# Attention's bias added by VectorE from tables with reversed keys, and the transfers around it in another order

## The chip, the cores and the metric

One core of a Trainium2 chip. The metric is the device time of one launch in microseconds (us), here the median of several runs. Engines: TensorE (matmuls, and weight loads beside them), VectorE, ScalarE, GpSimd, and SyncE, which issues most of the DMA transfers; ScalarE issues the others in its own instruction stream. The engines run side by side and order themselves by semaphores.

## The reference, cut to what matters

One layer of a streaming encoder for 256 prompt tokens and 32 sample tokens, width 1024, float32. Each group has its own conditioning vector c; `silu(c) @ w_ada + b_ada` gives six rows (shift, scale and gain, for the mixer and for the experts). The mixer projects `h = x * (1 + s1) + b1` with one matrix w_in (1024 x 2048) to three groups of heads:

```python
# A: 4 heads, chunks of 64, all earlier chunks in reach, clipped relative bias
logits = einsum(q, k) * HEAD_DIM**-0.5 + table[clip(rel, -128, 128) + 128]
logits = where(band_valid, logits, NEG_INF); p = softmax(logits); o = p @ v
# B: 8 query heads on 2 key heads, window of own chunk + 128 keys, sinks
logits = einsum(q, k) * HEAD_DIM**-0.5 + t5_table[t5_bucket(rel)]
m = max(max(logits), sink); e = exp(logits - m); p = e / (sum(e) + exp(sink - m))
# C: GLU, causal depthwise conv of width 31, LayerNorm, swish
```

The sample group attends to cached keys and values and its own 32. The groups' outputs go through w_out, then residual and LayerNorm. Keys, values and the end of the convolution's input are outputs too. Then comes a mixture of 32 experts (top 4 of 32, w_e_in 1024 x 2048 and w_e_out 1024 x 1024 for each expert, float32), residual and LayerNorm.

## The kernel before, in words

*The start.* SyncE issues twelve w_ada pieces of 2 MB (`ada_unit`, L369; six pairs of two halves, four ring slots at first, later two), w_in in five transfers on the other half of the big tile `w`, and small rows. After the first piece of each pair it issues b_ada as one transfer of 128 KB: each of four 256-column quarters copied to 32 partitions. TensorE multiplies a piece (`ada`, L1393), VectorE adds b_ada (`add_mod`, L923). The first four pieces give scale and shift of the mixer; they are transposed and put into `modc` by four chained copies (L954). Thirteen projections of 128 columns and three for the values follow (L1485); the other pieces of w_ada stand among them, the fifth after the sixth projection. VectorE runs the convolution beside this.

*The bias tables.* VectorE copies the transposed tables (L915), GpSimd extends them to rows of 512 relative positions (L538 to L541), ScalarE writes these to DRAM and reads them back in ten transfers with one element's shift a partition (L649 to L654): partition p holds the bias row beginning at element p. With keys in rising order the partitions come out in reversed order. So the bias enters the logits through a matmul: `anti` (a reversed identity; `anti32` for the sample, by blocks of 32) times the table (L1549, L1555), with start=True, and q*k is added on top of it in PSUM (L1553, L1564). GpSimd builds `anti` and `anti32` at the start.

*The attention.* 15 steps (`ATT`): for token tile 0 two of A and four of B (steps 0 to 5, 128 keys, two heads a step), the same for tile 1 (steps 6 to 11, 256 keys), and three for the sample (12 to 14, four heads in one tile). The text calls the first six short steps, the next six long steps. For one step the work goes: logits (TensorE) -> maxima (VectorE, L1062 or L1065) -> exps (ScalarE, L727, reads the logits in PSUM and writes `prob`, in `hb`) -> normalise (VectorE, L1087) -> transposes of the probabilities (TensorE, L1581) -> copy_pT (ScalarE, L740) -> values (TensorE, L1597) -> copy_o (VectorE, L1093). `prob` has two slots. The loops, each engine's instructions in this order:

```python
# TensorE: logits 0, 1, 2; then for s in 0..14:
#   transpose_p(s); logits(s+3) for s < 5, none for s = 5, logits(s+2) from 6; values(s); out_proj part from s = 6
# ScalarE: exps(0), exps(1); then copy_pT(s); exps(s+2)
# VectorE: maxima 0, 1, 2; normalise(0); then copy_o(s-1); normalise(s+1); maxima of the step whose logits came
```

The output projection (L1633) stands in parts among steps 6 to 14 (`OP_AFTER`), six matmuls of 512 columns (as two passes each where the profile counts them) in steps 6 to 9.

Before exps(0) ScalarE copies the last values, stores rows of the conditioning to DRAM (`store_mod`, L656), and then issues ten transfers: eight of values and keys (L702 to L710, shown as L700) and two of the convolution's end (L713).

*SyncE's order around it.* When all projections are done, four loads of expert 0 (`load`, L430, shown as L406); then a wait for the two transfers of the convolution's end, for st_mod and others; then six transfers that broadcast gain, scale and shift rows (L438, L440), four more loads of expert 0, and the copies of the caches to the outputs. Two loads of expert 1 follow when the attention is done, expert 0's w_e_out (L409) when the output projection is done, and more from then on, in a ring of 20 slots of 1 MB, as blocks of experts come to an end.

*The experts.* 51 blocks of 32 token slots: gather (L1746), w_e_in (L1766), activation, w_e_out (L1795), combine (L1729).

Of the kernel before, what the change touches and what calls it, by code (L numbers as in the profile page):

```python
# [10 lines left out]
ALU = mybir.AluOpType  # L11
ACT = mybir.ActivationFunctionType
AX_X = mybir.AxisListType.X
# [51 lines left out]
def hybrid_streaming_encoder_step(nc, x_prompt, x_sample, cache_a_k, cache_a_v, cache_b_k, cache_b_v, state_conv,  # L65
# [6 lines left out]
    with ExitStack() as ctx:  # L72
# [3 lines left out]
        def sem(name):  # L76
# [28 lines left out]
        prob = HB[:, 0:1024].rearrange("p (s h k) -> p s h k", s=2, h=2)  # L105
# [45 lines left out]
        anti = sb("anti", [P, P])  # L151
        anti32 = sb("anti32", [P, P])
# [64 lines left out]
        ld_ada = [sem(f"ld_ada{s}") for s in range(4)]  # L217
# [9 lines left out]
            sem(n) for n in ("warm_done", "csig_done", "csil_done", "cT_done", "scT_done"))  # L227
        small_done, small_used, tabs_ready = sem("small_done"), sem("small_used"), sem("tabs_ready")
# [10 lines left out]
        log_done, negm_done, exp_done, prob_done = (sem(n) for n in ("log_done", "negm_done", "exp_done", "prob_done"))  # L239
# [118 lines left out]
        def logits_free(s):  # L358

            return exps_through(s - 3 if s < 8 else (s - 2 if s < 14 else 10))  # L360
# [6 lines left out]
        def _(sp):  # L367

            def ada_unit(u):  # L369
                pair, half = divmod(u, 2)  # L370
                if u >= 4:
                    sp.wait_ge(ada_done, u - (3 if u < 6 else 1))
                sp.dma_start(ring[:, ada_slot(u)], w_ada[0, 512 * half:512 * (half + 1), D * pair:D * (pair + 1)]  # L373
                             .rearrange("(k p) n -> p k n", p=P)).then_inc(ld_ada[ada_slot(u)], 16)
                if half == 0:
                    if pair >= 2:
                        sp.wait_ge(mod_ready, pair - 1)
                    src = bass.AP(tensor=b_ada.tensor, offset=b_ada.offset + D * pair, ap=[[256, 4], [0, 32], [1, 256]])
                    sp.dma_start(bada[:, pair % 2, :], src).then_inc(ld_bada[pair % 2], 16)
# [50 lines left out]
            load(0, 0, 0, 4)  # L430
# [10 lines left out]
            load(0, 0, 4, 8)  # L441
# [59 lines left out]
        def _(pool):  # L501
# [14 lines left out]
            for tile in (anti, anti32):  # L516
                link(g.memset(tile[:, :], 0.0))
# [3 lines left out]
            link(g.affine_select(out=anti[:, :], in_=anti[:, :], compare_op=ALU.not_equal, fill=1.0, base=-(P - 1),  # L521
                                 pattern=[[1, P]], channel_multiplier=1))
            a32 = anti32[:, :].rearrange("p (b j) -> p b j", b=4)
            link(g.affine_select(out=a32, in_=a32, compare_op=ALU.not_equal, fill=1.0, base=-31,
# [78 lines left out]
        def _(eng):  # L603
# [112 lines left out]
            def exps(s):  # L716
# [4 lines left out]
                if s == 0:  # L721
                    eng.wait_ge(tr_used, J_Z + 2)
# [1135 lines left out]
```

## Time and profile before

| | us |
|---|---|
| median of 3 runs (lowest, highest) | 1267.29 (1265.98, 1271.55) |
| the profiled execution | 1268.6 |
| its span | 1266.9 |
| TensorE busy | 1027.2 (81%) |
| VectorE busy | 314.9 (25%) |
| ScalarE busy | 181.1 (14%) |
| GpSimd busy | 64.4 (5%) |
| mean granted TensorE clock | 0.923 |

Busy is the time in which the engine had an instruction under way; register work and the issuing of DMAs are not counted. The granted clock is a share of full speed: 1.00 is 2.4 GHz, 0.50 is 1.2 GHz. The span is the profiled execution's own, the rest of its time lies around it. The kernel reads 451.59 MB, 359 GB/s over the span.

### The profile page before, as it was taken

What the parts mean: (1) busy time and instruction counts of PE and PEld (TensorE: products, weight loads), DVE (VectorE), ACT (ScalarE), POOL (GpSimd) and SP (SyncE); (2) the same over time, 40 slices, a digit from 0 to 9 for tenths busy, and PEclk for the clock granted to TensorE, in tenths of its full rate; (3) what the DMA queues carried; (4) which work ended last, traced back from release to release, by engine and by line L of the source; (5) the groups of instructions that cost most, each with busy time, mean ns of one, the idle gap of its engine ahead of it and who ended that gap; (6) DMA issues with size and microseconds to landing.
All of it is one profiled execution on the core that took longest, in us unless ns stands there. A gap on an engine that the chain in (4) does not pass through costs nothing.

```text
span 1266.9 us, 30779 instructions
## 1 busy us (share of the span) xinstructions
PE 1027.2 (81%) x12329; PEld 484.9 (38%) x12330; DVE 314.9 (25%) x1021; ACT 181.1 (14%) x521; POOL 64.4 (5%) x142
## 2 busy tenths in 40 slices
PE   2789799798988778769788968997887897877973
PEld 1456554443443324224333424442433343332421
DVE  0286446611113112111211211121121121111215
ACT  0101333511111101011111101110110110110100
POOL 1820000000024000000000000000000000000000
PEclk9899899699998889989899989998898999888986
DMA  9997682879999999997998998099989989999994
GB/s 323 334 309 276 191 311 103 332 312 421 420 420 421 420 421 421 420 421 313 423 420 334 424 419 347 0 397 420 379 366 419 409 346 421 421 420 421 421 420 153
DMA packets 78409, 454.99 MB, mean 359 GB/s; under 512 B 9020, under 2 KB 17126, under 8 KB 29106
## 3 DMA queue, kind: packets, MB, share of 16 engines
q1 hardware_dynamic: 74092, 449.26, 87.5%
q10 hardware_dynamic: 4229, 4.41, 1.2%
q8 instruction: 74, 1.21, 0.4%
q14 instruction: 14, 0.11, 0.0%
HBM read 451.59 MB, written 2.61 MB: 359 GB/s over the span
## 4 chain that ended last, share of the span: by engine, by line
PE 41%; DMA 24%; SPq 22%; DVE 6%; issue 4%; ACT 1%; ACTq 1%; DVEq 0%
DMA w<-in_w_e_out 23%; PE bank L1766 15%; SPq L406 9%; PE bank L1795 8%; SPq L409 8%; PE bank L1746 3%; SPq L387 2%; PE comb L1729 2%; PE bank L1633 1%; PE comb L1633 1%; SPq L373 1%; PE bank L1783 1%; PE bank L1759 1%; DMA w<-in_w_ada 1%; DVE mt L1281 1%
## 5 line engine op out<-in xcount | busy, mean ns | idle before, releaser
L1766 PE MATMUL bank<-w,mt 128*32 128x512 f32 x3264 | 395.5, 628 | 51.9 <-DMA w<-in_w_e_in 51.7
L1795 PE MATMUL bank<-w,mt 128*32 128x256 f32 x3264 | 195.8, 385 | 47.0 <-DMA w<-in_w_e_out 32.9
L1766 PEld LDWEIGHTS bank<-w,mt 128*32 128x32 f32 x3264 | 96.8, 113 | 310.1 <-issue 209.3
L1273 DVE TENSOR_SCALAR mt<-bank 128x256 f32<-128x256 f32 x51 | 21.6, 424 | 696.7 <-PE bank L1766 696.7
L1795 PEld LDWEIGHTS bank<-w,mt 128*32 128x32 f32 x3264 | 98.3, 110 | 128.1 <-DMA w<-in_w_e_out 49.1
L1746 PE MATMUL bank<-pick,hb 128*128 128x32 bf16 x2448 | 79.2, 179 | 53.3 <-issue 53.0
L1746 PEld LDWEIGHTS bank<-pick,hb 128*128 128x128 bf16 x2448 | 74.9, 97 | 76.4 <-issue 76.0
L860 ACT ACTIVATE mt<-mt 128x256 f32<-128x256 f32 x51 | 21.3, 417 | 504.2 <-DVE mt L1273 504.2
L1729 PE MATMUL comb<-mt,gpickT 32*128 32x256 f32 x816 | 81.1, 471 | 0.5 <-ACT mt L869 0.5
L1747 PE MATMUL bank<-pick,hb 96*128 96x32 bf16 x408 | 72.4, 178 | 0.0
L1729 PEld LDWEIGHTS comb<-mt,gpickT 32*128 32x128 f32 x816 | 35.5, 204 | 51.3 <-issue 48.2
L869 ACT ACTIVATE mt<-bank 128x256 f32<-128x256 f32 x51 | 19.6, 384 | 233.3 <-PE bank L1795 233.3
L1747 PEld LDWEIGHTS bank<-pick,hb 96*128 96x128 bf16 x408 | 39.8, 98 | 0.0
L1783 PE MATMUL bank<-ident,mt 128*128 128x128 f32 x102 | 25.3, 330 | 17.2 <-DVE mt L1281 17.2
L1725 PE MATMUL bank<-mt,gpickT 128*128 128x256 f32 x102 | 39.1, 469 | 0.0
L985 DVE SCALAR_TENSOR_TENSOR w<-w,cwT 128x318 f32<-128x318 f32 x60 | 35.5, 591 | 2.3 <-DVE mt L934 0.2
L1314 DVE TENSOR_SCALAR pick<-iota,rkc 128x32 bf16 x150 | 27.4, 241 | 20.5 <-DVE gtc L1302 10.8
L1264 DVE TENSOR_SCALAR gpick<-iota,rkc,gtc 128x128 f32 (+1 forms) x102 | 32.4, 358 | 0.0
L862 ACT ACTIVATE gpickT<-bank 128x384 f32<-128x384 f32 x51 | 25.0, 491 | 41.5 <-PE bank L1779 41.5
L1783 PEld LDWEIGHTS bank<-ident,mt 128*128 128x128 f32 x102 | 16.2, 206 | 27.7 <-DVE mt L1281 27.6
L1522 PE MATMUL comb<-mt,w 128*128 128x288 f32 x80 | 22.2, 434 | 4.6 <-DVE mt L969 2.6
L1298 DVE TENSOR_SCALAR sel<-eye 96x32 bf16 (+1 forms) x31 | 5.5, 178 | 81.9 <-issue 81.9
(339 smaller groups left out, 814.7 us busy)
## 6 DMA issues: line engine op xcount, KB each, us to landing
w<-in_w_e_in SPq DMA_DIRECT2D x256, 1024.0 KB, 26.2
w<-in_w_e_out SPq DMA_DIRECT2D x128, 1024.0 KB, 21.5
w<-in_w_ada SPq DMA_DIRECT2D x12, 2048.0 KB, 11.3
w<-in_w_in SPq DMA_DIRECT2D x3, 2048.0 KB, 22.5
w<-in_w_in SPq DMA_DIRECT2D x2, 1024.0 KB, 20.9
w<-in_w_out SPq DMA_DIRECT2D x4, 512.0 KB, 10.2
w<-in_w_out SPq DMA_DIRECT2D x2, 1024.0 KB, 12.7
w<-mod_rows SPq DMA_DIRECT2D x4, 512.0 KB
```

The source lines that it names most:

```text
L406: sp.dma_start(slot[s], src).then_inc(ld_slot[s], 16)
L409: sp.dma_start(slot[s], src).then_inc(ld_slot[s], 16)
L985: link(v.scalar_tensor_tensor(out=yconv[:, c, :], in0=uext[:, c, w:w + Y_LEN], scalar=cwT[:, c, w:w + 1], in1=yconv[:, c, :], op0=ALU.mult ...
L1264: v.tensor_scalar(gpick[:, t, :, :], ids, rkc[:, t, :], gtc[:, t, :], ALU.is_equal, ALU.mult)
L1314: ins = v.tensor_scalar(pick[0:r, t, :], iota[0:r, bass.ds(first, SLOTS)], rkc[0:r, t, :], None, ALU.is_equal)
L1725: return mm(bank[7][:, 0:256], gpickT[:, 2 * P:3 * P], outb, start=False, stop=True, skip_group_check=True)
L1729: ins = mm(comb[:, q, c:c + 256], gpickT[r, P * t:P * (t + 1)], outb[r, :], start=False, stop=True, skip_group_check=True)
L1746: mm(out, hb[:, HB_AT[t], h, P * k:P * (k + 1)], pick[:, t, :], start=(t == 0 and h == 0), stop=False)
L1747: ins = mm(out, hb_s[0:96, P * k:P * (k + 1)], pick[0:96, 2, :], start=False, stop=True)
L1766: ins = mm(quarter(bank[0][SLOTS * q:SLOTS * (q + 1), :], 0), xT[:, SLOTS * k:SLOTS * (k + 1)], quarter(slot[s], q), start=False, stop=(k ...
L1783: ins = nc.tensor.transpose(bank[6][:, 256 + P * c:256 + P * (c + 1)], act.rearrange("p (d k) -> p k d", k=2)[:, c, :], ident[:, :])
L1795: ins = mm(bank[0][SLOTS * q:SLOTS * (q + 1), 0:256], hid, slot[s][:, D * (k % 2) + 256 * q:D * (k % 2) + 256 * (q + 1)], start=False, sto ...
```

## The change

Tables: the rows of relative positions are written in reversed order (L915, L538 to L541), and the transfers with a shift a partition begin at the other end (L649 to L654). Each partition then holds the bias of its own query, with the keys in reversed order. The three masks (L581 to L583) move with that. `anti` and `anti32` and all matmuls with them go; q*k is the only matmul of the logits. VectorE adds the bias, read backwards, to the logits while it moves them from PSUM to the probability slot, and takes the maximum there; exps works in place in SBUF. The probability slots are three, the third on what was `lnrow`. A bank of logits is free when VectorE has added (`log_used`), no longer when exps is through.

```diff
+        def probs_at(s):
+            at = (0, 512, 2880)[s % 3]
+            return HB[:, at:at + 512].rearrange("p (h k) -> p h k", h=2 if ATT[s][1] < 2 else 1)
+        def bias_of(s):
+            kind, t, j = ATT[s]
+            last = keys_of(kind, t) - 1
+            if kind == "A":
+                return bias_a[:, 2 * j:2 * j + 2, last::-1]
+            if kind == "B":
+                return bias_b.rearrange("p (n i) k -> p i n k", n=2)[:, j, :, last::-1]
+            return bias_sa[:, last::-1].unsqueeze(1) if kind == "SA" else bias_sb[:, j:j + 1, last::-1]
...
 (maxima, VectorE)
+                if s >= 3:
+                    dve.wait_ge(pT_done, s - 2)
-                    link(v.tensor_reduce(mx[:, 0:2], comb[:, first - 1:first + 1, 0:nk], AX_X, ALU.max))
+                    v.tensor_tensor(L, comb[:, first - 1:first + 1, 0:nk], bias, ALU.add).then_inc(log_used, 1)
                 else:
                     for h in range(nh):
-                        link(v.tensor_reduce(mx[:, h:h + 1], logit_part(s, h), AX_X, ALU.max))
+                        ins = v.tensor_tensor(L[:, h, :], logit_part(s, h), bias[:, h, :], ALU.add)
+                    ins.then_inc(log_used, 1)
+                dve.wait_ge(log_used, s + 1)
+                link(v.tensor_reduce(mx[:, 0:nh], L, AX_X, ALU.max))
 (exps, ScalarE)
-                if s >= 2:
-                    eng.wait_ge(pT_done, s - 1)
-                    a.activation(pr[:, h, 0:nk], logit_part(s, h), ACT.Exp, bias=stat[:, s % 3, h:h + 1],
+                    a.activation(pr[:, h, 0:nk], pr[:, h, 0:nk], ACT.Exp, bias=stat[:, s % 3, h:h + 1],
 (logits, TensorE)
-                    pe.wait_ge(exp_done, logits_free(s))
+                    pe.wait_ge(log_used, logits_free(s))
-                        mm(logit_part(s, h), anti[:, :], bias, start=True, stop=False, skip_group_check=True)
-                        ins = mm(logit_part(s, h), qkT[r, q, P * t:P * (t + 1)], qkT[r, k, 0:nk], start=False, stop=True, skip_group_check=True)
+                        ins = mm(logit_part(s, h), qkT[r, q, P * t:P * (t + 1)], qkT[r, k, 0:nk], start=True, stop=True)
```

ScalarE's output transfers: none ahead of exps(0) any more. An activation with Exp stands behind store_mod(5), and the ten issues go behind exps(s+2) of steps 0 to 4, two a step.

```diff
             store_mod(5, 3)
+            a.activation(warm[0:1, 0:1], warm[0:1, 1:2], ACT.Exp)
             eng.wait_ge(proj_used, NPROJ)
...
                 if s + 2 < NATT:
                     exps(s + 2)
+                if s == 0:
+                    send_conv()
+                elif s in (1, 2):
+                    send_values(s)
+                elif s in (3, 4):
+                    send_keys(s - 2)
```

SyncE: the fourth w_ada piece in two transfers of 1 MB, the second on a semaphore of its own, for which TensorE waits in the middle of the piece; b_ada as four transfers of 2 partitions each, on a tile that VectorE zeroes first; expert 0's first eight loads together, behind the broadcasts.

```diff
+                if u == 3:
+                    for h in range(2):
+                        sp.dma_start(ring[:, 3, 2 * h:2 * h + 2], w_ada[0, 512 + 256 * h:768 + 256 * h, D:2 * D]
+                                     .rearrange("(k p) n -> p k n", p=P)).then_inc(ld_ada[(3, 4)[h]], 16)
...
                 if half == 0:
+                    sp.wait_ge(bada_zero, 1)
...
-                    sp.dma_start(bada[:, pair % 2, :], src).then_inc(ld_bada[pair % 2], 16)
+                    for q in range(4):
+                        at = D * pair + 256 * q
+                        sp.dma_start(bada[32 * q:32 * q + 2, pair % 2, :], b_ada[0:1, at:at + 256].to_broadcast([2, 256]))\
+                          .then_inc(ld_bada[pair % 2], 16)
...
             sp.wait_ge(proj_done, NPROJ)
-            load(0, 0, 0, 4)
             sp.wait_ge(ust_sent, 32)
...
-            load(0, 0, 4, 8)
+            load(0, 0, 0, 8)
```

VectorE: `modc` is written by two copies without a chain between them, instead of four chained ones (L952 to L956).

## Rows read from the trace of the kernel before

**Rows 1.** The page's chain that ended last: shares by engine.
```profile
PE 41%; DMA 24%; SPq 22%; DVE 6%; issue 4%; ACT 1%; ACTq 1%; DVEq 0%
```

**Rows 2.** TensorE's timeline: start, us, line, operation, shape, idle before and releaser.
```profile
37.31 3.49 PE L1402 MATMUL comb<-w,scT 128*32 128x256 f32 x32 [2.54 <-DMA w<-in_w_ada]
...
75.60 3.33 PE L1402 MATMUL bank<-w,scT 128*32 128x256 f32 x32 [3.60 <-DMA w<-in_w_ada]
...
140.40 0.68 PE L1549 MATMUL comb<-w,anti 128*128 128x128 f32 x4 [1.07 <-DVE mt L1045]
```

**Rows 3.** SyncE's timeline: when it issued what, and how long that held it.
```profile
50.90 5.36 SPq L390 DMA_DIRECT2D hb<-in_ln_g  x1
...
64.28 0.43 SPq L373 DMA_DIRECT2D w<-in_w_ada  x1
...
100.86 10.14 SPq L373 DMA_DIRECT2D w<-in_w_ada  x2
...
140.26 2.97 SPq L406 DMA_DIRECT2D w<-in_w_e_in  x4
167.98 0.33 SPq L438 DMA_DIRECT2D w<-mod_rows  x1
...
217.87 2.17 SPq L409 DMA_DIRECT2D w<-in_w_e_out  x4
```

**Rows 4.** Windows of 20 us: busy time (instructions) by engine, clock, DMA share, GB/s.
```profile
20.00:40.00 20.00, 14.09 (x146) 8.18 (x148) 1.28 (x5) 0.00 (x0) 7.09 (x76) 0.85 1.04 377
...
80.00:100.00 20.00, 20.00 (x181) 11.98 (x183) 18.63 (x36) 1.65 (x4) 0.00 (x0) 1.00 0.83 299
...
140.00:160.00 20.00, 14.30 (x74) 10.38 (x76) 9.40 (x46) 7.49 (x33) 0.00 (x0) 0.67 0.99 298
```

**Rows 5.** The chain in order of time: start, us, what. Around the attention, and after.
```profile
145.54 0.42 ACTq L713
146.05 1.28 ACT L727
...
148.93 0.69 PE bank L1581 x2
...
164.89 0.66 PE bank L1581 x4
...
278.73 25.05 DMA w<-in_w_e_out
```

**Rows 6.** ScalarE's timeline: the issues of values and keys.
```profile
140.28 4.75 ACTq L700 DMA_DIRECT2D out<-w  x8
```

**Rows 7.** VectorE's timeline: before the first maxima, and a maximum of either size.
```profile
140.26 0.74 DVE L1050 COPY nsink_s<-nsink 32x2 f32<-32x2 f32 x4
...
154.08 0.42 DVE L1062 TENSOR_REDUCE mx<-comb 128x2 f32<-128x256 f32 x1 [1.02 <-PE comb L1553]
...
160.80 0.69 DVE L1062 TENSOR_REDUCE mx<-comb 128x2 f32<-128x512 f32 x1 [1.90 <-PE comb L1553]
```

**Rows 8.** Groups by line, 137 to 218 us: a two-operand instruction of 512 elements.
```profile
L1106 DVE TENSOR_TENSOR mt<-bank,w 128x512 f32<-128x512 f32 x2 | 1.4, 687 | 0.0
```

**Rows 9.** The page's groups: ScalarE from SBUF, and from PSUM.
```profile
L860 ACT ACTIVATE mt<-mt 128x256 f32<-128x256 f32 x51 | 21.3, 417 | 504.2 <-DVE mt L1273 504.2
...
L869 ACT ACTIVATE mt<-bank 128x256 f32<-128x256 f32 x51 | 19.6, 384 | 233.3 <-PE bank L1795 233.3
```

**Rows 10.** Windows with a low clock, columns as in rows 4.
```profile
149.00:157.00 8.00, 8.00 (x40) 5.99 (x42) 4.05 (x20) 3.53 (x18) 0.00 (x0) 0.50 1.05 330
...
238.00:242.20 4.20, 4.20 (x24) 0.92 (x20) 2.04 (x10) 0.20 (x1) 0.00 (x0) 0.50 1.02 429
```

**Rows 11.** The chain in a long step: bias, output projection, the next bias.
```profile
170.85 0.86 PE comb L1549 x4
...
172.93 2.77 PE bank L1633 x6
...
176.14 0.86 PE comb L1549 x4
```

More of the change, by code:

```diff
@@ L216, in hybrid_streaming_encoder_step @@
         ld_win = [sem(f"ld_win{j}") for j in range(4)]
-        ld_ada = [sem(f"ld_ada{s}") for s in range(4)]
+        ld_ada = [sem(f"ld_ada{s}") for s in range(5)]
         ld_bada = [sem("ld_bada0"), sem("ld_bada1")]
@@ L238, in hybrid_streaming_encoder_step @@
         keys_ready = sem("keys_ready")
-        log_done, negm_done, exp_done, prob_done = (sem(n) for n in ("log_done", "negm_done", "exp_done", "prob_done"))
+        log_done, log_used, negm_done, exp_done, prob_done = (
+            sem(n) for n in ("log_done", "log_used", "negm_done", "exp_done", "prob_done"))
         pT_done, pT_copied, o_done, o_copied = (sem(n) for n in ("pT_done", "pT_copied", "o_done", "o_copied"))
@@ L925, in add_mod @@
                 dve.wait_ge(ada_done, 2 * pair + 2)
-                dve.wait_ge(ld_bada[pair % 2], 16 * (pair // 2 + 1))
+                dve.wait_ge(ld_bada[pair % 2], 64 * (pair // 2 + 1))
+                dve.wait_ge(bada_zero, 1)
                 if pair >= 4:
@@ L952, in _ @@
             for g in range(2):
-                for h in range(2):
-                    ins = v.tensor_copy(modc[:, :, g, :].rearrange("p a (q h) -> p a h q", h=2)[:, :, h, :], pv[:, :, h, :, g])
-                    if (g, h) != (1, 1):
-                        link(ins)
+                ins = v.tensor_copy(modc[:, :, g, :].rearrange("p a (q h) -> p a h q", h=2), pv[:, :, :, :, g])
             ins.then_inc(modc_done, 1)
@@ L1400, in ada @@
                     k = 4 * half + q
+                    if u == 3 and q == 2:
+                        pe.wait_ge(ld_ada[4], 16)
                     for j in range(4):
@@ L1563, in logits @@
                             q, keys = qkT[r, 4 + h, SEQ:NTOK], kbT_s[r, :]
-                        ins = mm(ps[32 * h:32 * h + 32, 0:nk], q, keys, start=False, stop=True, skip_group_check=True)
+                        ins = mm(ps[32 * h:32 * h + 32, 0:nk], q, keys, start=True, stop=True)
                 ins.then_inc(log_done, 1)
@@ L1627, in out_proj @@
                     else:
-                        pe.wait_ge(exp_done, exps_through(11))
+                        pe.wait_ge(log_used, 12)
                 for n in range(first, last):
@@ L1631, in out_proj @@
                     if t == 1 and n == DK:
[L1632 removed]
+                        pe.wait_ge(log_used, 13)
                     ins = mm(bank[OP_BANKS[t][j]][:, :], hT[:, k, P * t:P * (t + 1)], w2v[:, k, 512 * j:512 * (j + 1)],
```

89 lines of the change are left out of this document (40 added, 49 removed).

## The prediction

> **What bounds the kernel now.** I read the page's chain first, then the windows of all engines, then the chain and each engine's timeline around the attention. The chain that ended last is 41% TensorE, 24% DMA and 22% SyncE's queue [rows 1]: no engine bounds the whole. Three stretches have different bounds. (a) To 75.6 us the input stream: TensorE stands idle 3.60 us before the fifth w_ada piece [rows 2], which SyncE could issue only at 64.28, after a train of small transfers of which one alone held its queue 5.36 us [rows 3]. (b) From 80 us to the end of attention mostly TensorE, busy 20.00 of 20 us from 80 to 100; but from 140 to 160 only 14.30 [rows 4], because the first exponentials waited behind ten output transfers that ScalarE issued [rows 5]. (c) From 276 us the chain changes between TensorE and expert weights; the first long piece is a transfer of 25.05 us at 278.73 [rows 5]. SyncE issues expert 0's tail at 217.87, released by the end of the output projection [rows 3], and every later load by a block's progress. So what comes off stretches (a) and (b) should move (c) as a whole.
>
> **The change part by part.**
>
> *b_ada as 8 small transfers instead of 2 large ones, fourth piece halved.* Before the fifth w_ada piece two transfers of 128 KB fall away. The input stream runs at 377 GB/s [rows 4], so 0.26 MB are 0.7 us. The added issues (three more for each pair, one for the half) stand in a queue that the stream throttles anyway (one issue of 5.36 us), and so for the later pairs, where two w_ada issues held the queue 10.14 us [rows 3]. Uncovered, three more short issues would cost 1.5 us a pair. The fourth piece: today TensorE starts at 37.31 after 2.54 us idle and works 3.49 us [rows 2]; with half the data there before, half of that, 1.75 us, goes ahead. modc in two copies rather than four chained ones saves some tenths. That makes some 3 us up to the first projection, but it all ends at 75.6: TensorE would only wait 6 us instead of 3.60 for the fifth piece [rows 2]. What is late next is that piece, so the worth of the group is 0.7 us. Bounds: +0.5 (an issue delays the piece) to -3.6 (the whole idle goes). I take **-0.7**, nearest to the bytes.
>
> *Output transfers moved off ScalarE's queue ahead of exps(0), Exp table loaded early.* Today: last issue at 145.54, table load 1.28 at 146.05, first transposes of probabilities at 148.93 [rows 5]. After: store_mod ends at 140.28, where the eight issues of the values and keys begin [rows 6], the table load and one tiny activation end near 141.8. VectorE is through with its nsink copies at 141.0 [rows 7]. TensorE begins step 0 at 140.40 [rows 2]; without bias matmuls the logits are there at 140.9. VectorE then needs for each of steps 0, 1, 2 the added add (0.45, as the 256-element instructions beside it), the maximum (0.42 [rows 7]) and the small ones: 1.0, 1.05 and 1.3, to 144.45; normalise(0) is queued behind them, 0.65. Transposes at 145.1 instead of 148.93: **-3.8**. The adds cost 1.4 of the 5.3 us that the moved issues and the table free. Bounds: -2.5 (reversed operand at half speed, 3 x 0.4) to -4.5.
>
> *Bias added by VectorE, short steps 0 to 5.* Today 148.93 to 164.89, 2.66 us a step [rows 5], TensorE-bound: transposes, bias, q*k and values at the low clock. Without the bias TensorE needs 2.0. VectorE today has 1.8 a step (maximum 0.42 [rows 7], two small, copy of o, three for normalise); with the add 2.24, and for steps 6 and 7, whose maxima fall here, 0.54 more each, since a 512-element maximum is 0.69 [rows 7] and a product of two 512-element operands 0.69 [rows 8]. ScalarE has 1.2 a step plus two issues: the eight took 4.75 in all [rows 6], 0.95 to 1.5 a pair. Going through both queues by hand, ScalarE reaches copy_pT(5) at 158.5 and VectorE normalise(6) at 158.95; transposes(6) at 159.5. That is 14.4 us against 15.96: **-1.6**. What is late next is ScalarE's queue: copy_pT, which TensorE's values wait for, stands behind the two issues. Bounds: -3.9 (TensorE's own 2.0 a step) to +2.0 (each of the eight at about twice its length, see rivals). The new waits on pT_done and log_used name work done a step earlier. That `exp` reads SBUF costs 0.03 (0.417 against 0.384 for 256 elements [rows 9]).
>
> The Trainium skill (VectorE: DVE Perf Modes, the section on the TRN2 errata) says that VectorE and ScalarE pay a fixed extra per instruction when the source is SBUF. By its ScalarE row that is some 43 ns an exp, 1.2 us over the 27; the trace shows 33 ns, and by it 0.9 us, spread over an engine that is idle most of each long step.
>
> *The clock at the change from short to long steps.* Today TensorE's clock fell to its lower level (1.2 GHz, granted 0.50) after the idle before 148.9, and stayed there from 149 to 157 although TensorE was busy 8.00 of 8 us [rows 10]; the steps from 160 on ran at 2.4. After the change an idle of 3.2 us remains (logits(2) end 141.9, transposes 145.1), and the short steps hold less matmul work. I expect the low level until the output projection has begun in step 6. In the only dense cold start at hand the clock was low for 4.2 us of dense weights [rows 10]. Step 6: transposes, logits and values cold about 3.0 us instead of 1.66, and some 3 us of out_proj at half speed: 1.3 + 1.4, **+2.7**. Bounds 0 and +5.
>
> The Trainium skill (TensorE: Matmul & The Clock Gate, the section What's actually happening) says that throttled is the default state and that activity releases the throttle. It speaks against taking matmuls away next to an idle stretch. By a plain reading, busy means released, the short steps would be warm soon and the +2.7 nothing; the trace here disagrees, busy 8.00 of 8 us and still 0.50.
>
> *Bias, long steps 6 to 14.* One step today: bias 0.86, out_proj 2.77, and transposes, q*k and values 1.66, from one bias to the next 5.29 [rows 11]. TensorE is the bound: logits run two steps ahead. Without bias 4.43, and 0.1 comes back because values now start when copy_pT (0.60) ends. VectorE then has 3.2 a step, ScalarE 2.0: cover is left. Four such steps (logits 8 to 11): 4 x 0.76 = 3.0; the sample's biases in steps 10 and 11, 0.49 and 0.37 less the same wait: 0.7. In step 12 to 14 TensorE waits for ScalarE, nothing gained. **-3.7**, bounds -2 (VectorE's reversed reads at double length still fit) to -4.7.
>
> *Expert 0's first loads after the conv outputs and the row broadcasts.* Today four are issued at 140.26 and the broadcasts only at 167.98, since the conv outputs landed late behind those loads [rows 3]. After: conv outputs sent near 148, broadcasts near 151, and with 10 MB at 377 GB/s [rows 4] all is there by 178. The broadcasts, first in line, are read after step 11, the weights after 217.87 less 7. Nothing, with 30 us to spare. GpSimd without anti: nothing, it idles.
>
> **Sum**: -0.7 - 3.8 - 1.6 + 2.7 - 3.7 = -7.1. The profiled run took 1268.6 (span 1266.9 and 1.7 around it): 1261.5. That run lies 1.3 above the median of the runs shown, 1267.29, so on the median's scale **1260.2**.
>
> **Rivals.**
> 1. *The clock does not hurt* (returned by step 6, as it did today at 160, or never fell). For: today it came back in the short steps. Against: today a 256-column bias ran just then, now gone. Without the +2.7: 1257.5.
> 2. *ScalarE's queue takes the place of TensorE.* Eight issues among the steps, beside the row and weight loads. For: between weight streams one small issue of SyncE took 5.36 [rows 3]. Against: these eight took 0.59 each on the mean beside such loads [rows 6]. At twice the length the short steps lose their 1.6 and 2.0 more: 1263.8.
> 3. *Hidden anyway*: expert weights set the pace and the earlier start is given back as a longer wait in (c). For: DMA is 24% of the chain. Against: all loads from 207 us on are released by attention and block events. 1267.
> 4. *Slower: the low clock lasts into the long steps.* Place: steps 6 to 11. For: 8 us of full work at 0.50 [rows 10]. Each long step would take 8.3 instead of 4.43, 3.9 more; past 2.5 such steps the 9.8 us of other gains are gone; all six give 1257.5 + 23 = 1280. Against: the 4.2 us for 512-column work [rows 10].
>
> **How the numbers follow.** Forecast 0.50, rival 1 0.22, rival 2 0.17, rival 3 0.06, rival 4 0.05. A difference under 0.5% (6.3 us, below 1261.0) can't be told from none by this measurement. Faster by more: two thirds of the forecast's cases (1260.2 with 2 either way), nearly all of rival 1, little of rival 2: 0.55. Slower: rival 4 and a remnant, 0.06. The same: 0.39. The range 1255.6 to 1264.8 takes in rivals 1 and 2 and a somewhat larger gain in (a).
>
> **What would show it.** Right: transposes of step 0 near 144.4 (3.8 and 0.7 earlier); six short steps of 2.4 with VectorE or ScalarE ending the waits; clock 0.50 into step 6; long steps of 4.5; no waits for VectorE's maxima there; the w_e_out transfer of 278.73 some 7 us earlier. Wrong: a gap before w_ada's fifth piece that closed (then -3 in (a)), adds well over 0.45 and 0.69 (reversed reads cost), long steps over 5 us, or a chain after 276 that isn't shifted.

## The result, and the profile after

The changed kernel takes 1255.35 us (median of 5 runs, 1253.86 to 1259.88) beside 1267.29 of the kernel before: the ratio is 0.9899, 95% interval 0.9883 to 0.9916. That is 11.9 us less where 7.1 were forecast, just below the range. The two repeats below gave 1257.02 and 1257.1, inside the range, but beside a kernel before of 1268.6 and 1268.5: 11.6 and 11.4 us less, so the gain is larger than forecast in all three. The profiled execution has a span of 1252.3 us at a mean granted clock of 0.912. The chain has nearly kept its shares [rows 1]:

```profile
PE 41%; DMA 25%; SPq 20%; DVE 7%; issue 5%; ACT 1%; DVEq 0%
```

TensorE's timeline (columns as in rows 2), where the input stream's part ends, where attention begins, and then transposes of probabilities of steps 5 to 8 and 12, with the first part of the output projection:

```profile
71.23 1.93 PE L1437 MATMUL bank<-w,scT 128*32 128x256 f32 x32 [1.98 <-DMA w<-in_w_ada]
...
134.61 0.72 PE L1584 MATMUL comb<-w 64*128 64x128 f32 x8 [1.11 <-DVE mt L1071]
...
150.35 0.69 PE L1608 MATMUL bank<-ident,hb 128*128 128x128 f32 x2
152.72 1.12 PE L1608 MATMUL bank<-ident,hb 128*128 128x128 f32 x4
155.97 3.92 PE L1660 MATMUL bank<-w,mt 128*128 128x512 f32 x6
159.73 0.60 PE L1608 MATMUL bank<-ident,hb 128*128 128x128 f32 x4
...
164.28 0.60 PE L1608 MATMUL bank<-ident,hb 128*128 128x128 f32 x4
...
180.78 0.49 PE L1608 MATMUL bank<-ident,hb 128*128 128x128 f32 x3
```

The same view of the kernel before, steps 7, 8 and 12:

```profile
170.25 0.60 PE L1581 MATMUL bank<-ident,hb 128*128 128x128 f32 x4
175.54 0.60 PE L1581 MATMUL bank<-ident,hb 128*128 128x128 f32 x4
...
193.87 0.49 PE L1581 MATMUL bank<-ident,hb 128*128 128x128 f32 x3
```

The chain of the kernel after, in order of time: the first transposes, VectorE's add and maximum of step 3 and of step 6 (the first with 512 elements), which stand on the chain, and the first long transfer of expert weights:

```profile
139.61 0.69 PE bank L1608 x2
...
141.07 0.44 DVE hb L1092
141.53 0.43 DVE mx L1098
...
147.73 0.61 DVE hb L1092
148.36 0.70 DVE mx L1098
...
265.00 26.02 DMA w<-in_w_e_out
```

Between these marks lie the differences of the two profiled executions, to be compared with the terms of the sum:

| stretch | before | after | difference | predicted |
|---|---|---|---|---|
| to the first logits | 140.40 | 134.61 | -5.8 | -0.7 |
| first logits to transposes(0) | 8.53 | 5.00 | -3.5 | -3.8 |
| short steps 0 to 5 | 15.96 | 13.11 | -2.8 | -1.6 |
| step 6 | 5.36 | 7.01 | +1.6 | +2.7 |
| steps 7 to 11 | 23.62 | 21.05 | -2.6 | -3.7 (steps 6 to 14) |
| to the first long w_e_out transfer | 84.86 | 84.22 | -0.6 | 0 |
| from there to the end of the span | 988.2 | 987.3 | -0.9 | 0 |
| span | 1266.9 | 1252.3 | -14.6 | -7.1 |

The profiled run after lies 1.3 us below its median and the one before 1.3 above: that is the rest between 14.6 and 11.9. Read in the last two rows: what the front gains, the experts keep. The other rows compare one profile with one; how far a stretch differs between profiles of the same kernel is told with the repeats below, and it is up to 2 us in the short steps and 4 us ahead of the first logits.

In these windows (columns as in rows 4) the clock falls ahead of the first transposes and is low until step 6's output projection is under way, busy though TensorE is:

```profile
136.00:140.00 4.00, 0.39 (x2) 0.29 (x2) 3.41 (x15) 1.76 (x8) 0.00 (x0) 0.71 0.99 227
140.00:144.00 4.00, 4.00 (x22) 2.17 (x20) 3.10 (x13) 2.48 (x12) 0.00 (x0) 0.50 1.02 220
144.00:148.00 4.00, 4.00 (x21) 1.94 (x19) 3.69 (x19) 2.60 (x12) 0.00 (x0) 0.50 1.01 230
148.00:152.00 4.00, 3.04 (x14) 1.33 (x12) 3.79 (x13) 2.08 (x7) 0.00 (x0) 0.50 1.08 367
152.00:156.00 4.00, 3.91 (x21) 2.29 (x21) 2.54 (x9) 1.48 (x5) 0.00 (x0) 0.50 1.00 227
156.00:160.00 4.00, 4.00 (x11) 1.94 (x10) 1.92 (x8) 1.19 (x5) 0.00 (x0) 0.73 1.05 319
```

The groups by line and shape, 134 to 185 us (out<-in, shapes, count | busy, mean ns of one | idle before): the reversed reads cost nothing, since an add of 512 elements takes as long as a plain one [rows 8] and as the maximum beside it.

```profile
L1092 DVE TENSOR_TENSOR hb<-comb,w 128x512 f32<-128x512 f32 x6 | 4.1, 690 | 4.1 <-PE comb L1584 4.1
L1098 DVE TENSOR_REDUCE mx<-hb 128x2 f32<-128x512 f32 x6 | 4.1, 686 | 0.2
...
L1092 DVE TENSOR_TENSOR hb<-comb,w 128x256 f32<-128x256 f32 x4 | 1.7, 424 | 0.8 <-PE comb L1584 0.7
...
L748 ACT ACTIVATE hb<-hb,stat 128x128 f32<-128x128 f32 x12 | 4.7, 392 | 0.8 <-DVE stat L1101 0.7
```

In ScalarE's timeline (columns as in rows 6) the moved issues lie over the activations of the same engine, 0.3 to 0.5 us each, where rows 6 gave 0.59 on the mean:

```profile
142.39 0.40 ACTq L714 DMA_DIRECT2D out<-w  x1
142.59 0.39 ACT L748 ACTIVATE hb<-hb,stat 128x128 f32<-128x128 f32 x1
142.83 0.48 ACTq L714 DMA_DIRECT2D out<-w  x1
```

### The profile page after: what moved, and what is told of

The parts are those of the page before. It is cut to its first block, busy times and chain, and to the rows that moved or that the text cites. A ratio compares the mean times of both kernels' runs of the same rounds, so it can differ in the third digit from the quotient of the medians.

```text
span 1252.3 us, 30692 instructions
## 1 busy us (share of the span) xinstructions
PE 1018.4 (81%) x12275; PEld 476.4 (38%) x12276; DVE 320.2 (26%) x1035; ACT 182.7 (15%) x522; POOL 63.4 (5%) x138
## 4 chain that ended last, share of the span: by engine, by line
PE 41%; DMA 25%; SPq 20%; DVE 7%; issue 5%; ACT 1%; DVEq 0%
DMA w<-in_w_e_out 24%; PE bank L1793 16%; SPq L428 9%; PE bank L1822 8%; SPq L431 6%; PE bank L1773 3%; SPq L409 3%; PE comb L1756 2%; PE bank L1660 1%; PE comb L1660 1%; PE bank L1810 1%; PE bank L1786 1%; DMA w<-in_w_ada 1%; DVE mt L1314 1%; DVE mt L1310 1%
## 5 line engine op out<-in xcount | busy, mean ns | idle before, releaser
L1347 DVE TENSOR_SCALAR pick<-iota,rkc 128x32 bf16 x150 | 26.4, 236 | 19.1 <-DVE gtc L1335 11.8
```

## The experiments

Every kernel of this section, unless another base is named, is the kernel after with the edit that is shown; each also reads the experts' ends into a register by another instruction (`value_load` in place of `reg_load`), which by the first of them costs nothing. The kernel before ran beside them in four groups, with medians of 1268.6, 1268.5, 1268.9 and 1268.5; ratios are to those. "Piece" is the start of the fifth w_ada piece on TensorE.

**The yardsticks.** The two kernels again with the common edit.

> The kernel before with one edit that every kernel of this series has: the ends of the first two experts' loops are read with bounds (value_load) instead of reg_load. Both theories: the milestones of the trace of before come back: first projection at 44.6 us, fifth w_ada piece on TensorE at 75.6, logits of step 0 at 140.4, transposes of step 0 at 148.9, of step 6 at 164.9; total within 0.3% of before. If the fifth piece moves by more than 1 us by itself, a single profile can't tell the parts of the start apart.

> The changed kernel with the same edit. Milestones of the trace of after come back: first projection 40.5, fifth piece 71.2, logits 134.6, transposes 139.6 and 152.7; total 10 to 14 us under before.

> The kernel after once more, beside the two others on the same chip, for a direct comparison: 0.991 of the kernel before, 1255 to 1257, first logits near 134, transposes(12) near 180.

Measured: before 1268.58, ratio 1.0001 (0.9986 to 1.0015); after 1257.02, 0.9914 (0.9883 to 0.9945), and 1257.1, 0.9913 (0.9896 to 0.9929). Piece 76.47, 70.39 and 70.15; first logits 144.26, 133.79 and 133.52. Step 6 took 5.74 and 5.75 in the two, not 7.01. Five kernels below have this attention unchanged and another start or other transfers; in four of them it took 7.03 to 7.21, in one 5.93. So the loss at step 6 varies from profile to profile, and 7.01 is no exception. The kernel before varies too. In its repeat the granted clock was 0.57 from 128 to 136, the first logits came 3.9 us later than in the first profile, and the short steps took 13.83 us instead of 15.96, with the clock back at 1.00 from step 3 on (steps 0 and 6 in TensorE's timeline):

```profile
152.58 0.69 PE L1581 MATMUL bank<-ident,hb 128*128 128x128 f32 x2 [5.09 <-DVE hb L1087]
...
166.41 0.66 PE L1581 MATMUL bank<-ident,hb 128*128 128x128 f32 x4 [0.19 <-DVE hb L1087]
```

In the two experiments that follow, whose attention is the old one, the short steps took 16.09 and 14.91. With the new attention they took 13.10 to 13.12 in all eight profiles that leave it unchanged.

**Which part makes the front 5.8 us shorter?** On the kernel before, b_ada's small transfers alone, and the halved fourth piece alone:

```diff
-                    src = bass.AP(tensor=b_ada.tensor, offset=b_ada.offset + D * pair, ap=[[256, 4], [0, 32], [1, 256]])
-                    sp.dma_start(bada[:, pair % 2, :], src).then_inc(ld_bada[pair % 2], 16)
+                    for q in range(4):
+                        at = D * pair + 256 * q
+                        sp.dma_start(bada[32 * q:32 * q + 2, pair % 2, :], b_ada[0:1, at:at + 256].to_broadcast([2, 256]))\
+                          .then_inc(ld_bada[pair % 2], 16)
```

> Before with b_ada alone changed (four transfers of 2 partitions a pair instead of one of 128 partitions). Theory A (the prediction failed because a 128 KB broadcast transfer costs the stream far more than its bytes): the fifth piece starts on TensorE 3 us or more earlier, at 72.5 or before, and the total falls by 3.5 to 6 us. Theory B (the gain came from the fourth piece in halves and the earlier modulation rows): the fifth piece stays within 1 us of 75.6, total within 1.5 us of before.

```diff
+                if u == 3:
+                    for h in range(2):
+                        sp.dma_start(ring[:, 3, 2 * h:2 * h + 2], w_ada[0, 512 + 256 * h:768 + 256 * h, D:2 * D]
+                                     .rearrange("(k p) n -> p k n", p=P)).then_inc(ld_ada[(3, 4)[h]], 16)
```

> Before with the fourth w_ada piece alone in two halves. Theory A: the first projection comes 1.5 to 2 us earlier (42.6 to 43), the fifth piece stays within 1 us of 75.6, total as before. Theory B: the fifth piece comes 3 us or more earlier and the total falls by 3.5 us or more.

Measured: b_ada alone 1264.43, 0.9961 (0.9945 to 0.9977), piece at 70.50. The halved piece alone 1270.01, 1.0009 (0.9990 to 1.0028), piece at 76.14. TensorE's row for it in each:

```profile
70.50 1.94 PE L1408 MATMUL bank<-w,scT 128*32 128x256 f32 x32 [1.53 <-DMA w<-in_w_ada]
```

```profile
76.14 3.64 PE L1409 MATMUL bank<-w,scT 128*32 128x256 f32 x32 [6.39 <-DMA w<-in_w_ada]
```

So b_ada's transfers carry it, 4.1 us, and the halved piece is hidden by the wait for the fifth, as predicted (6.39 us of idle where some 6 were forecast). The rows show a second thing: with b_ada alone the piece ran in 1.94 us, not 3.64. In six profiles of all 17 the idle before it was 1.53 to 2.05 us, and it took 1.93 or 1.94; in the eleven others the idle was 3.60 to 6.39, and it took 2.80 to 3.64, as at the lower level of the clock. The small b_ada transfers do not decide which: of the twelve profiles that have them and no further copied rows, all with the piece at 70.07 to 72.27, six are of the one kind and six of the other.

**Why do 0.26 MB cost 4 us?** Two more transfers of 128 KB, read by nobody, behind the first two b_ada loads, on a tile of their own. First four rows of 1 KB, each read by 32 partitions, as b_ada was before; then as many bytes with a row for each partition; then 16 different KB, each read by 8 partitions. The three differ in a second thing as well: the outermost count of the source's access pattern is 4 in the first, 128 in the second and 16 in the third.

```diff
+                    if pair < 2:
+                        sp.dma_start(spare[:, pair, :], bass.AP(tensor=b_ada.tensor, offset=b_ada.offset + D * pair, ap=[[256, 4], [0, 32], [1, 256]])).then_inc(spare_done, 16)
...
+                        sp.dma_start(spare[:, pair, :], w_in[0, 128 * pair:128 * pair + 128, 0:256]).then_inc(spare_done, 16)
...
+                        sp.dma_start(spare[:, pair, :], bass.AP(tensor=b_ada.tensor, offset=b_ada.offset, ap=[[256, 16], [0, 8], [1, 256]])).then_inc(spare_done, 16)
```

> The changed kernel, and in the places of the first two b_ada transfers one transfer more each, of 128 KB to 128 partitions of a spare tile that nothing reads, with b_ada's old pattern (32 partitions read the same 1 KB of DRAM). Theory A1 (many readers of the same kilobyte make the transfer slow): the loss comes back, the fifth piece starts on TensorE 3.5 us or more later than in the changed kernel (71.2 and 70.4 in its two profiles), and more than with rows of their own. Theory A2 (128 small packets cost that, whatever they read): the same loss as with rows of their own. Theory A3 (only the bytes count): 0.7 us later.

> The changed kernel with the same two additional transfers, but each partition reads 1 KB of its own from w_in. Theory A1: at most 1.5 us later at the fifth piece. Theory A2: as many us later as with the same row, 3.5 or more. Theory A3: 0.7 us later in both.

> The kernel after, with two more 128 KB transfers in the same place as in c1_extra_same_row and c2_extra_own_rows, but here 16 different KB are read, each by 8 of the partitions (c1: one KB read by 32 partitions at a time, 4 us lost; c2: each partition its own row, nothing lost). If the loss goes with the number of readers of one KB: the fifth w_ada piece starts on TensorE between 71.0 and 75, nearer to 72, and the total is 1257 to 1259. If any row read more than once costs the same: 75 and 1260.7 as c1. If 8 readers are free: 71.0 and 1256.6 as c2.

| readers of one KB | piece | its issue by SyncE | median | ratio to before |
|---|---|---|---|---|
| 32 | 74.90 | 64.37 | 1260.67 | 0.9945 (0.9925 to 0.9964) |
| 8 | 73.06 | 61.36 | 1258.64 | 0.9923 (0.9903 to 0.9942) |
| 1 | 70.98 | 60.59 | 1256.59 | 0.9916 (0.9897 to 0.9934) |
| (no extra transfer, first repeat) | 70.39 | 60.77 | 1257.02 | 0.9914 (0.9883 to 0.9945) |

The bytes are the same in the first three (454.59 MB for the whole kernel). In SyncE's timeline of the 32 readers and of the single ones (columns as in rows 3) the issues behind the second extra transfer are held 5 us longer; the windows of both, under them, show less input with 32 readers in the stretches where the copied rows arrive:

```profile
14.25 10.12 SPq L391 DMA_DIRECT2D w<-in_w_ada  x2
24.42 27.39 SPq L413 DMA_DIRECT2D w<-in_w_in  x5
```

```profile
12.09 4.82 SPq L391 DMA_DIRECT2D w<-in_w_ada  x2
16.96 31.43 SPq L413 DMA_DIRECT2D w<-in_w_in  x5
```

```profile
12.00:16.00 4.00, 0.00 (x0) 0.00 (x0) 0.00 (x0) 0.00 (x0) 0.00 (x0) 1.00 1.06 310
...
28.00:32.00 4.00, 2.29 (x25) 1.20 (x29) 1.29 (x5) 0.00 (x0) 1.23 (x5) 0.84 1.04 301
```

```profile
12.00:16.00 4.00, 0.00 (x0) 0.00 (x0) 0.00 (x0) 0.00 (x0) 0.00 (x0) 1.00 1.04 370
...
28.00:32.00 4.00, 3.87 (x69) 2.01 (x64) 1.29 (x5) 0.00 (x0) 1.16 (x4) 1.00 1.02 394
```

The DMA engines are as busy in both (1.06 and 1.04 with 32 readers, 1.04 and 1.02 with one), yet bring 16% and 24% less with 32. So the cost does not go by bytes: it is some 2 us a transfer of the first pattern, by the piece (3.9 us for two) and by the median (4.1). With 8 readers the fifth piece is issued 0.8 us later than with one, where 32 readers make it 3.8; its start on TensorE at 73.06 is just outside the 70.07 to 72.27 of the twelve profiles named above, and the total can't be told from either neighbour by its interval.

Is it the readers, or the outermost count? The pages count the packets of the first repeat of the kernel after, and of the kernels with 32 readers, with one and with 8:

```profile
DMA packets 77732, 454.33 MB, mean 363 GB/s; under 512 B 9059, under 2 KB 16445, under 8 KB 28425
DMA packets 77996, 454.59 MB, mean 361 GB/s; under 512 B 9067, under 2 KB 16709, under 8 KB 28689
DMA packets 78020, 454.59 MB, mean 362 GB/s; under 512 B 9091, under 2 KB 16733, under 8 KB 28713
DMA packets 78021, 454.59 MB, mean 361 GB/s; under 512 B 9092, under 2 KB 16734, under 8 KB 28714
```

Each adds the 256 packets of 1 KB; the small ones beside them are 8 with 32 readers and 32 or 33 with the others, 4 against 16 a transfer. The times of single packets, as the same traces record them, fit that. The first copied transfer's stretch over 5.5 us, those with a row each over 2.8. Of the first copied transfer never more than 4 of the 1 KB packets are under way at once (of the second 5, for 0.03 us), in the kernel before as well; with a row each it is up to 7 and 10, with 8 readers up to 8 and 12. A packet takes 65 and 66 ns with 32 readers, 46 with one and 46 to 48 with 8. As an estimate from these, 128 packets of 65 ns, four at a time, are 2.1 us; that is the cost measured. So the transfer with 32 readers looks cut into four parts, each of which works through 32 packets in line while the large transfers behind it wait for the slowest part, and the outermost count of 4 explains more than the readers do. This was not run by itself: no kernel here has 32 readers of one KB in a pattern that begins with 16 or more. The readers' own share, the step from 46 to 65 ns among it, stays open.

**What is the bias change worth?** All of the change but the bias: anti, two probability slots, the matmuls and `exp` from PSUM as before.

```diff
-                    v.tensor_tensor(L, comb[:, first - 1:first + 1, 0:nk], bias, ALU.add).then_inc(log_used, 1)
+                    link(v.tensor_reduce(mx[:, 0:2], comb[:, first - 1:first + 1, 0:nk], AX_X, ALU.max))
...
+                        mm(logit_part(s, h), anti[:, :], bias, start=True, stop=False, skip_group_check=True)
```

> The changed kernel's transfers, table load and order of SyncE and ScalarE, but the bias still added by matmuls, with the probabilities in two slots and exps reading PSUM (before's attention). By the terms of the prediction: first transposes 5.2 us sooner after the logits began than before (8.5 us then, so 3.3), as VectorE has no adds; short steps as before at 2.7 us, long steps 5.3. So about 2.5 to 4 us over the changed kernel in total. Rival (the bias matmuls were hidden behind VectorE and ScalarE anyway): within 1.5 us of the changed kernel.

Measured: 1256.21, 0.9924 (0.9894 to 0.9954), against 1257.02 and 1257.1 with it. Its windows and the steps from 0 on in TensorE's timeline:

```profile
140.00:144.00 4.00, 4.00 (x37) 2.82 (x36) 3.25 (x17) 2.99 (x17) 0.00 (x0) 1.00 1.05 221
144.00:148.00 4.00, 3.97 (x26) 2.50 (x24) 3.48 (x16) 2.66 (x13) 0.00 (x0) 1.00 1.01 249
```

```profile
139.12 0.44 PE L1608 MATMUL bank<-ident,hb 128*128 128x128 f32 x2 [1.70 <-DVE hb L1112]
...
140.73 0.44 PE L1608 MATMUL bank<-ident,hb 128*128 128x128 f32 x2
...
150.13 0.66 PE L1608 MATMUL bank<-ident,hb 128*128 128x128 f32 x4 [0.19 <-DVE hb L1112]
```

TensorE idles only 1.70 us before transposes(0), the clock stays at 1.00, steps 0 and 1 with their bias matmuls take 1.61 each (3 and 4, with the logits of steps 6 and 7, 2.24), and steps 0 to 5 take 11.0 us, 5.0 less than in the first profile before (2.8 less than in its repeat) and 2.1 less than after the whole change. The first transposes were expected 3.3 us behind the first logits and came 4.93 behind them, no sooner than the 5.00 with VectorE's adds: the bias matmuls keep TensorE on the first three logits for 3.2 us, and VectorE's maxima wait for them. From the first logits to transposes(12) it is 44.9 us; 46.2, 44.9 and 44.9 in the three profiles of the whole change; 53.5 and 51.1 in the two of the kernel before. What the bias saves in the long steps is paid in the short ones.

**Is it the clock, or VectorE?** Matmuls that nothing reads: four of 512 columns between the last early logits and the first transposes; or these and one of 256 columns ahead of the logits of steps 3 to 7.

```diff
+                if 3 <= s < 8:
+                    mm(bank[logit_banks(s)[0]][:, 0:256], ident[:, :], W1[1][:, 8192:8448], start=True, stop=True)
...
+            for n in range(4):
+                mm(bank[6][:, :], ident[:, :], W1[1][:, 8192:8704], start=True, stop=True)
```

> The changed kernel with the four unread 512-column matmuls between the logits of step 2 and the first transposes, and none in the steps. Theory E1 (the idle stretch alone brought the clock down): clock 1.00 through the short steps, step 6 4.5 to 4.7 us, as with matmuls in the steps too. Theory E2 (the thin short steps bring it down by themselves): clock 0.50 again before step 6, and step 6 takes 5.5 us or more.

> The changed kernel with matmuls whose results nothing reads: four of 512 columns between the logits of step 2 and the first transposes, and one of 256 columns ahead of the logits of steps 3 to 7. Theory C (the low clock costs at the change to the long steps, 2.7 us by the prediction): the granted clock stays 1.00 through the short steps, step 6 takes 4.5 to 4.7 us from transposes to transposes instead of 7.0 (5.7 in the second profile), and the first w_e_in group is not changed; total 1 to 3 us under the changed kernel. Rival (the low clock is hidden, or the added matmuls cost what it gives): transposes of step 7 no earlier than 0.5 us before the changed kernel's, counted from the transposes of step 0.

Measured: the four alone 1255.26, 0.9910 (0.9885 to 0.9934); all of them 1254.43, 0.9892 (0.9875 to 0.9908). With all, the granted clock is 1.00 from 140 to 160, and steps 0, 6 and 7 begin in TensorE's timeline with

```profile
140.99 0.44 PE L1610 MATMUL bank<-ident,hb 128*128 128x128 f32 x2 [0.42 <-DVE hb L1120]
...
153.97 0.66 PE L1610 MATMUL bank<-ident,hb 128*128 128x128 f32 x4 [0.19 <-DVE hb L1120]
...
158.58 0.60 PE L1610 MATMUL bank<-ident,hb 128*128 128x128 f32 x4
```

The short steps take 13.0 us even at 1.00 (13.1 at 0.50): steps 2 to 6 each begin after a wait for VectorE. Step 6 takes 4.61. So VectorE holds the short steps, and the low clock's whole price is step 6, 2.4 us in the first profile, 1.1 in the repeats, 1.3 to 2.6 in the five other profiles with this attention; in the median the gain is within the noise. With the four alone the clock fell later all the same, at some 144 us, among the thin short steps, and step 6 took 5.72: the idle stretch ahead of them is not needed for it.

**Both together.** The bias stays on TensorE in steps 0 to 5 (identity times the reversed table) and is added by VectorE from step 6 on; then the same with two unread matmuls of 512 columns ahead of the logits of steps 6 and 7.

```diff
+                    if s < 6:
+                        for h in range(2):
+                            mm(logit_part(s, h), ident[:, :], bias_of(s)[:, h, :], start=True, stop=False, skip_group_check=True)
...
+                if s in (6, 7):
+                    for n in range(2):
+                        mm(bank[logit_banks(s)[n]][:, :], ident[:, :], W1[1][:, 8192:8704], start=True, stop=True)
```

> The changed kernel, but in the six short steps the bias enters by a matmul again (identity times the reversed table) and exps reads PSUM; long steps and sample keep the add on VectorE. Theory D (in the short steps the bias matmuls stand in time TensorE has anyway and keep its clock at the upper level, while the adds make VectorE the bound; in the long steps the adds are hidden): short steps take 11.0 us in all, as in the kernel with all but the bias, long steps 4.55 as in the changed one, clock 1.00 throughout; from the first logits to the transposes of step 12 some 41.5 us against 46.3 in the changed kernel and 44.9 with all but the bias. So 4 to 5 us under the changed kernel. Rival (the clock falls anyway, or VectorE in steps 3 and 4 is the bound): 44 us or more, total within 2 us of the changed kernel.

> d1_hybrid (TensorE and the copy ahead as before the change in the short steps up to 5, the new bias from step 6 on) with two matmuls of 512 columns, which nothing reads, ahead of the logits of steps 6 and 7. Theory: the bias change's saving in the long steps is paid back by VectorE in the short steps and by the low granted clock in step 6; with both taken away, transposes(6) come as in d1 (about 11.7 us behind transposes(0)), the clock stays at 1.00, step 6 takes 4.6 us instead of 5.5 to 7.0, and from the first logits to transposes(12) it is about 42 us (after: 45 to 46.2; all but the bias 44.9; d1 44.1). The total is then some 2 to 3 us below the kernel after. Rival: the clock is not what makes step 6 long, then step 6 stays at 6 us and the total equals d1.

Measured: 1257.21, 0.9916 (0.9895 to 0.9936), and 1257.04, 0.9921 (0.9893 to 0.9950). No better than the kernel after. The first had 44.1 us from the first logits to transposes(12): steps of 1.6 to 1.8 until VectorE's adds for steps 6 and 7 fell among them, then 2.5, the clock fell, and step 6 took 6.55. The second was to mend that. Its profiled execution took 1269.03, 11.8 us more than the first one's. Of this 3.7 lie ahead of the attention, with the clock at 0.65 and 0.50 from 124 to 132; 8.0 lie between the first logits and transposes(12). There the clock fell again at some 142, among the first logits and ahead of the idle of 1.57 us before step 0 (in the first hybrid, with an idle of 1.58, it was still at 1.00), and with the bias on TensorE a short step at that level is 2.83 us:

```profile
147.10 0.69 PE L1628 MATMUL bank<-ident,hb 128*128 128x128 f32 x2 [1.57 <-DVE hb L1131]
...
149.92 0.69 PE L1628 MATMUL bank<-ident,hb 128*128 128x128 f32 x2
```

Of its six runs, four took 1253.5 to 1257.7 and two 1266.6 and 1269.0; the kernel with all but the bias has two at 1268.0 and 1268.4 among ten. None of the 15 runs of the changed kernel is above 1260.6, and none of the 28 of the seven others with all biases on VectorE above 1263.0. So the bias on VectorE gains nothing in the median but may take away a dependence on the clock. Only one such long run has a profile, and a third of its excess lies ahead of the attention; for the others this reading is argued, not shown.

**The other moves.** Output transfers back ahead of exps(0), with the bias on VectorE; and expert 0's first four loads back ahead of the broadcasts:

```diff
+            for t in (1, 2):
+                send_values(t)
+            for t in (1, 2):
+                send_keys(t)
+            send_conv()
```

> The changed kernel with the ten output transfers back ahead of exps(0) (the Exp table is still loaded before them). Prediction's term: the first transposes were 5.0 us after the first logits; with ten issues of 0.44 to 1.03 us ahead (5.7 in all today) exps(0) starts near 141.5 instead of 136.4, VectorE's adds are hidden under them: first transposes 8.5 us after the first logits, total 3 to 4 us over the changed kernel. Rival (they cost as much among the steps): within 1 us.

```diff
+            load(0, 0, 0, 4)
             sp.wait_ge(ust_sent, 32)
...
-            load(0, 0, 0, 8)
+            load(0, 0, 4, 8)
```

> The changed kernel with expert 0's first four loads back ahead of the wait for the convolution's outputs. Both by the prediction's step (worth nothing, 30 us to spare): milestones of the attention within 0.3 us, total within 1.5 us of the changed kernel. Rival: they slow the output issues of ScalarE (up to 1.03 us each beside the loads in the kernel before), and the short steps take 1 us or more longer.

Measured: outputs first 1259.94, 0.9938 (0.9917 to 0.9959), an interval that overlaps those of the kernel after, transposes(0) 7.00 us behind the first logits instead of 5.00 (8.5 were expected); loads early 1257.72, 0.9915 (0.9894 to 0.9936), no difference.

## Why the prediction was wrong

1. **b_ada as small transfers: the step that failed.** It was priced by bytes, 0.26 MB at 377 GB/s [rows 4], at 0.7 us; it measured 4.1 us by itself. What the runs show in its place is a price by the transfer: about 2 us for each of this pattern instead of 0.35, most likely because it goes in four parts only; that part of the cause is argued from the packet counts and times, not shown by a run of its own. In the profiles the fifth piece comes 4.37 us earlier. A further 1.40 come from the piece itself, 1.93 us instead of 3.33 at full rate, after an idle of 1.98 instead of 3.60; together 5.8. The second part is luck of the first profile and its two repeats: with the same b_ada transfers six of twelve profiles have it. The bound of -3.6, "the whole idle goes", held the six projections ahead of the piece where they were, though the text itself had them 3 us earlier; they moved too. The text called for a sign, a gap before the fifth piece that closed; it shrank from 3.60 to 1.98. The hint was in rows 3, one issue held for 5.36 us, and in a window of the kernel before, while the second copy of b_ada was under way:

```profile
28.00:32.00 4.00, 1.36 (x9) 0.62 (x13) 0.25 (x1) 0.00 (x0) 0.00 (x0) 0.84 1.03 306
```

   The same window of the kernel after has 392 GB/s.
2. **Output transfers and table: right in size, -3.5 for -3.8.** But its worth hangs on the rest: with the bias on TensorE it also keeps the clock up and is worth 8.2 us (1264.43 with b_ada alone, 1256.21 with all but the bias; the halved piece and the loads are nothing). With the bias on VectorE it is 2.8 to 2.9 (1259.94 against the two repeats, with intervals that overlap).
3. **Short steps: right direction, -2.8 for -1.6** in the first profiles, but -0.7 between the repeats, since the kernel before varies (13.83 to 16.09 in four profiles of its attention, 13.1 in all eight of the new one). ScalarE was taken for the limit, with its issues at 0.5 to 0.75 us each; they overlap its activations and hold nothing. VectorE is the limit: 2.0 us a step, and 2.4 where a 512-element add and maximum fall in (at the low clock TensorE is as full, but the steps are no shorter when it is at 1.00). Rival 2 is refuted.
4. **The clock into step 6: the mechanism as predicted**, 0.50 until the output projection is under way. The table's +1.6 for step 6, and +0.4 in the two repeats, have the bias's 0.8 already taken off; against the 4.61 of a step 6 at full rate the clock costs 2.4 and 1.1, for the +2.7 of the sum, and 2.4 to 2.6 in four further profiles. So the term was near the upper end of what happens, and rival 1, the clock doesn't hurt, is the case in none of the eight profiles. The rule of the Trainium skill weighed there (TensorE: Matmul & The Clock Gate, What's actually happening) taken plainly fails again: TensorE was busy 4.00 of 4 us from 140 to 148 and granted 0.50.
5. **Long steps: 4.55 for 5.30, three times**, and 3.70 for 4.05 once: -2.6. The price of a step was right (0.74 for 0.76). The sum had four such steps, but step 6's is counted in point 4, and the sample's biases gave 0.35 rather than 0.7.
6. **Shifted whole:** the first long w_e_out transfer comes 13.7 us earlier and the end 14.6. Rival 3, hidden anyway, is refuted, and so is rival 4: steps 7 on are at full rate. Expert 0's loads cost nothing, as predicted.

The forecast of the bias change itself as these terms have it, +1.4 for the adds ahead of the first transposes (inside the -3.8), short steps -1.6, clock +2.7, long steps -3.7, sums to -1.2; measured, all against all but it, it is +0.8 to +0.9 by the medians, within the noise. The 1.4 was not there, since the bias matmuls hold the first logits up by as much (4.93 against 5.00). That the outputs alone would already have freed the short steps was not seen, because each term was set against the kernel before and not against the kernel with the other parts in.

## What to carry to other kernels

Do not price a small broadcast load in a busy stream by its size. Look at its access pattern, at the packets that the page counts for it and at how many of them are under way at once; if only few rows are needed, load these and let the engines see zeros elsewhere. Repeat the profile of both kernels before a stretch is compared: here the kernel before moved by 2 us in the short steps by itself. Price the parts of a change against each other too: where one part keeps TensorE's clock up, another part that takes matmuls away may be worth nothing. After a stage is moved earlier, look which engine's own instructions fill a step; keeping the clock up does nothing where that engine is VectorE.

## What was unexpected of the hardware

- A transfer of 128 KB in 1 KB packets cost about 2 us more when its source pattern was 4 rows with 32 readers each than when each partition read its own, at nearly the same DMA busy share, with at most 4 or 5 of its packets under way at once instead of 7 and 10.
- VectorE reads an operand backwards at no cost: 690 ns for an add of 512 elements, where a plain one took 687 [rows 8]; 424 for 256.
- `exp` of 128 elements took 392 ns from SBUF; one from PSUM took 365 in the kernel before, 27 ns less:

```profile
L727 ACT ACTIVATE hb<-comb,stat 128x128 f32<-128x128 f32 x8 | 2.8, 365 | 0.0
```

- The granted clock stayed at 0.50 from 140 to 156, though TensorE was busy 14.95 of the 16 us with matmuls of 128 and 256 columns, and came back within the first part of the output projection with 512 columns; the fifth w_ada piece ran in 1.93 or 1.94 us after idles of 1.53 to 2.05 us and in 2.80 to 3.64 after 3.60 and more.
